# Delta rule's inverse in a two-layer recurrent kernel: each head in its own row half, products on the two diagonal quarters of TensorE, one transpose per level on VectorE

## The chip, the cores and the metric

The kernel runs on one core of a Trainium2 chip. The time is that of the whole kernel on the device, in microseconds (us). Before the change it is 2453.71 us, the median of three runs (2449.43, 2453.71, 2456.01).

## What is computed

Two layers of a mixer work on 1280 tokens (256 of context, 1024 of the latent) of width 1024. The change is in one stage of the first layer, the recurrence called rwkv: 8 heads of 64 channels, each with a 64x64 state that is decayed, corrected by a rank-one term and extended at every token, once forward and once backward over the tokens. The part of the reference:

```python
def rwkv_scan(inputs, S):
    def step(S, xs):
        r, v, kk, w, k, a = xs
        sa = jnp.einsum('bhvk,bhk->bhv', S, -kk)
        S = S * w[:, :, None, :] + sa[..., None] * (kk * a)[:, :, None, :] + v[..., None] * k[:, :, None, :]
        return S, jnp.einsum('bhvk,bhk->bhv', S, r)
    S, ys = lax.scan(step, S, tuple(jnp.moveaxis(t, 2, 0) for t in inputs))
    return jnp.moveaxis(ys, 0, 2), S
```

## The kernel before

The kernel doesn't step token by token. It cuts the tokens into 20 chunks of 64 (`C = 64`), and for each chunk, head and direction it forms a 64x64 strictly triangular matrix of key products, and needs the inverse of the identity plus that matrix. With the inverse a whole chunk is solved by one product per head. Two directions by 20 chunks give 40 steps; two steps (lanes 0 and 1) make a block, so `stage_rwkv_scan` (from L1540) runs over `B = 20` blocks. The 8 heads are `J = 4` pairs: head `q = 0` of a pair has its channels and chunk rows in partitions 0 to 63, head `q = 1` in 64 to 127. A block so holds 2 lanes x 4 pairs x 2 = 16 inverses of 64x64, all float32.

**The inverse by levels.** The inverse is grown in place in the tile `inv`. GpSimd sets blocks of two tokens (`begin_inverse`, L1990, four instructions a block). Then five levels (`TOP = 5`, `n` from 1 to 5) join neighbouring blocks of 2^n tokens into blocks of twice the size. A level is:

1. `half_product` (L1833) on TensorE: for each of the 16 inverses the strict matrix (`strict_t`, stationary, 64x64) times the 32 columns of the inverse that are to change (moving, 64x32). ScalarE copies the result from PSUM to the tile `half` (`copy_half`, L1903).
2. Beside it, `turn_inverse` on VectorE transposes the present inverse within blocks of 32x32 into the tile `lower` (L2047, L2049).
3. `upper_product` (L1842) on TensorE: `lower` (stationary, 64x64) times `half` (moving, 64x32).
4. `merge_upper` (L2055) on VectorE writes the result from PSUM into `inv` where a mask has ones. Only then may the next level's `half_product` and `turn_inverse` begin.

**Where the heads lie.** A matmul with 64 rows and 64 columns uses one quarter of the array: the rows are those of its operands' partitions, the columns those of its output's partitions. Before the change `inv` has a side index (`(j % 2) ^ q`), heads are taken two pairs at a time (`fours`), and the list `quarters` sends four consecutive matmuls to the four quarters: two of them keep the row half, two cross to the other one. `half` and `lower` hold heads in the crossed half between the two products, and `turn_inverse` has three instructions: one over 128 partitions for the side that stays, and two over 64 partitions that move the other side to the opposite half. The products lie in two PSUM banks, 32 of every 128 columns.

**The order of the work.** Each engine's order is written out by hand, and engines wait on semaphores. On TensorE the two products of a level have other work between them: the previous block's chunks (`begin_chunk` L1789, `solve_chunk` L1798, `begin_outputs` L1807, `update` L1815, `end_outputs` L1821), the next block's products (`strict_products` L1732, `products` L1743), `pull` (L1780), and transposes (`turn_keys` L1755, `turn_v` L1770). ScalarE has the copies out of PSUM (`copy_half`, `copy_u` L1926, `copy_y` L1943, and others), VectorE the masked products (`read_products` L2039), `add_rest` (L2064) and `update_state` (L2072, L2073). `update` waits for `copy_u`, which waits for `solve_chunk`. SyncE loads the next blocks' operands as the levels go by, waiting for `half_ready` and `upper_ready`.

A float32 matmul stands in the trace as two weight loads and two matmuls, so 16 matmuls are 32 rows of each kind.

Of the kernel before, what the change touches and what calls it, by code (L numbers as in the profile page):

```python
# [19 lines left out]
P = 128  # L20
# [559 lines left out]
R_LEVELS = 6  # L580
# [959 lines left out]
def stage_rwkv_scan(p, arena, operands, v_dram, shared, spare, own, chunk_decay, y, next_weights, free, bonus_dram):  # L1540
# [55 lines left out]
    with ExitStack() as local:  # L1596
# [4 lines left out]
        strict_t = sb("strict_t", [P, 2, 2, J, C])  # L1601
        inv = sb("inv", [P, 2, 2, 2, J // 2, C])
        lower = sb("lower", [P, 2, J, C])
        half = sb("half", [P, 2, J, C // 2])
        rest, pulled = sb("rest", [P, J, C]), sb("pulled", [P, 2, J, C])
# [14 lines left out]
            [P, 2 * J, C >> (n + 1), 1 << n])  # L1620
        identity = column(0, 5 + R_LEVELS).unsqueeze(1).broadcast_to([P, 2, J // 2, C])
        PAIR, KEYS, TURN, STRICT, CHAIN, OUT = 0, (2, 5), 3, 5, 6, 7
# [4 lines left out]
        flat = lambda a: a.rearrange("p l j n -> p (l j) n")  # L1627
        fours = [(lane, jj) for lane in range(2) for jj in range(J // 2)]
        quarters = [(0, 0), (1, 1), (0, 1), (1, 0)]
        four = lambda lane, jj: lane * (J // 2) + jj  # L1630
        own_inverse = lambda b, lane, j, q: inv[part(q), b % 2, (j % 2) ^ q, lane, j // 2, :]
        pair_bank = lambda which, lane, jj: bank(PAIR + which)[:, four(lane, jj) * P:four(lane, jj) * P + C // 2]
        pair_banks = p.psum[:, PAIR:PAIR + 2, :].rearrange("p r (f n) -> p (r f) n", n=P)[:, :, 0:C // 2]
        with nc.Block() as block:
# [88 lines left out]
            def _(pe):  # L1723
# [101 lines left out]
                def half_product(b, n):  # L1825
                    if n == 1:
                        pe.wait_ge(strict_read, 2 * (b + 1))
                        pe.wait_ge(level0_ready, 4 * (b + 1))
                    if b or n > 1:
                        pe.wait_ge(upper_merged, TOP * b + n - 1)  # L1830
                    for lane, jj in fours:
                        for q, r in quarters:
                            last = nc.tensor.matmul(pair_bank(q, lane, jj)[part(r)], strict_t[part(q), b % 2, lane, 2 * jj + r, :],  # L1833
                                                    changed(own_inverse(b, lane, 2 * jj + r, q), direction(b), n), start=True, stop=True)
                    last.then_inc(half_ready, 1)

                def upper_product(b, n):
                    pe.wait_ge(lower_turned, TOP * b + n)
                    pe.wait_ge(half_copied, TOP * b + n)
                    for lane, jj in fours:  # L1840
                        for q, r in quarters:
                            last = nc.tensor.matmul(pair_bank(q ^ r, lane, jj)[part(q)], lower[part(r), q ^ r, four(lane, jj), :],  # L1842
                                                    half[part(r), q, four(lane, jj), :], start=True, stop=True)
                    last.then_inc(upper_ready, 1)
# [53 lines left out]
            def _(act):  # L1898
                def copy_half(b, n):
                    act.wait_ge(half_ready, TOP * b + n)  # L1900
                    if b or n > 1:
                        act.wait_ge(upper_ready, TOP * b + n - 1)
                    nc.scalar.copy(half[:, :, :, :].rearrange("p q f n -> p (q f) n"), pair_banks).then_inc(half_copied, 1)  # L1903

# [74 lines left out]
            def _(pool):  # L1979
                begun, added = [0], [0]  # L1980

                def begin_inverse(b, lane, q):
# [3 lines left out]
                    if begun[0] >= 2:  # L1986
                        pool.wait_ge(level0_ready, begun[0] - 1)
                    begun[0] += 1
                    pairs = prod[part(q), b % 2, lane, q, :, part(q)].rearrange("p (j r) n -> p r j n", r=2)
                    nc.gpsimd.tensor_tensor(inv[part(q), b % 2, :, lane], pairs if q == 0 else pairs[:, ::-1],  # L1990
                                            identity[part(q)], ALU.add).then_inc(level0_ready, 1)
# [34 lines left out]
            def _(dve):  # L2026
# [14 lines left out]
                def turn_inverse(b, n):  # L2041
                    if n == 1:
                        dve.wait_ge(level0_ready, 4 * (b + 1))
                    if b or n > 1:
                        dve.wait_ge(upper_merged, TOP * b + n - 1)
                    here = inv[:, b % 2].rearrange("p s l j n -> p s (l j) n")
                    nc.vector.transpose(lower[:, 0], here[:, 0])  # L2047
                    for q in range(2):
                        last = nc.vector.transpose(lower[part(1 - q), 1], here[part(q), 1])  # L2049
                    last.then_inc(lower_turned, 1)  # L2050

                def merge_upper(b, n):
                    dve.wait_ge(upper_ready, TOP * b + n)
                    whole = inv[:, b % 2].rearrange("p s l j (g t w) -> p (s l j) g t w", t=2, w=1 << n)
                    nc.vector.copy_predicated(whole[:, :, :, 1 - direction(b)], added_to_pairs(direction(b), n),  # L2055
                                              pair_banks.rearrange("p f (g w) -> p f g w", w=1 << n)).then_inc(upper_merged, 1)

# [1898 lines left out]
```

## Time and profile before

| what | value |
|---|---|
| median of three runs | 2453.71 us |
| profiled execution, its own time | 2456.63 us |
| span of its core, first to last instruction | 2454.8 us |
| mean granted TensorE clock | 0.970 of full speed |
| TensorE busy (matmul) | 2294.7 us, 93% |
| VectorE busy | 1320.0 us, 54% |
| ScalarE busy | 794.4 us, 32% |
| GpSimd busy | 251.0 us, 10% |

The stage of the change runs from about 925 to 1305 us of the span. Busy time counts overlapping instructions once, and a matmul's row lasts from its start to its last result, so a TensorE that is busy need not start a matmul at its fastest rate. PE is TensorE's matmul, PEld its weight load, DVE VectorE, ACT ScalarE, POOL GpSimd. "issue" as the reason of a wait is idle time for which the profile shows no releaser. L1833 is line 1833 of the kernel.

### The profile page before, as it was taken

The page shows a single profiled execution, that of the slowest core. Times are in us where ns is not written, and L with a number is a line of the kernel's source. Part 1 is how long each engine was busy: PE and PEld are TensorE (multiplying, and loading weights), DVE is VectorE, ACT ScalarE, POOL GpSimd, SP SyncE. Part 2 cuts the span into 40 slices and gives each one's busy share as a digit, 9 for nine tenths or more (in the row PEclk, how much of TensorE's full clock was granted, in tenths as well). Part 3 has the DMA queues.
Part 4 walks back from the last instruction along what each step waited for, and adds up shares of the span by engine and source line. Part 5 has one row for each costly group of instructions (what it writes and reads, how often), then busy time and mean ns, then how long its engine had stood idle before and what let it go on. Part 6 is the DMA issues. An engine that isn't in the chain of part 4 may idle for free. (4 is left out here: it accounts for less than half of the span.)

```text
span 2454.8 us, 50670 instructions
## 1 busy us (share of the span) xinstructions
PE 2294.7 (93%) x22140; PEld 1417.6 (58%) x22140; DVE 1320.0 (54%) x2181; ACT 794.4 (32%) x1533; POOL 251.0 (10%) x280
## 2 busy tenths in 40 slices
PE   6999999999989988888887998999998999999898
PEld 4444456666644447887784443444685666756443
DVE  3320335553348756777774454555395666667514
ACT  4121222224455653443232222110101445465411
POOL 0000000000002211111221102341100000000000
PEclk8999999999989998999999998999999999999999
DMA  8100122122056654433325422111122100000233
GB/s 332 60 19 7 43 78 76 63 66 73 19 154 145 172 155 112 118 94 95 90 61 196 138 98 76 47 47 34 69 104 80 36 27 27 28 18 10 96 97 117
DMA packets 131866, 207.29 MB, mean 84 GB/s; under 512 B 15629, under 2 KB 95245, under 8 KB 128062
## 3 DMA queue, kind: packets, MB, share of 16 engines
q1 hardware_dynamic: 118398, 154.74, 20.2%
q0 software_dynamic: 13248, 49.32, 7.0%
q8 instruction: 175, 2.87, 0.5%
q14 instruction: 45, 0.37, 0.1%
HBM read 154.01 MB, written 50.01 MB: 83 GB/s over the span
## 5 line engine op out<-in xcount | busy, mean ns | idle before, releaser
L737 PE MATMUL psum<-arena,shared 128*128 128x512 f32 (+1 forms) x864 | 328.3, 524 | 1.5 <-PEq L223 1.5
L2861 PE MATMUL psum<-arena,second_shared 128*128 128x512 f32 (+1 forms) x640 | 282.3, 568 | 11.1 <-PEq L3682 6.4
L737 PEld LDWEIGHTS psum<-arena,shared 128*128 128x128 f32 x864 | 156.9, 191 | 108.5 <-issue 101.5
L2861 PEld LDWEIGHTS psum<-arena,second_shared 128*128 128x128 f32 x640 | 112.4, 195 | 77.0 <-issue 71.8
L1243 PE MATMUL psum<-shared,arena 128*128 128x512 f32 x320 | 150.0, 618 | 0.0
L2247 PE MATMUL psum<-shared,fin_mix 128*128 128x512 f32 x320 | 143.4, 601 | 2.9 <-POOL fin_mix L2380 2.9
L2247 PEld LDWEIGHTS psum<-shared,fin_mix 128*128 128x128 f32 x320 | 59.8, 192 | 75.0 <-issue 71.5
L1243 PEld LDWEIGHTS psum<-shared,arena 128*128 128x128 f32 x320 | 60.3, 196 | 73.3 <-issue 72.9
L841 ACT ACTIVATE shared<-psum 128x512 f32<-128x512 f32 (+1 forms) x48 | 25.2, 525 | 216.2 <-PE psum L737 216.2
L1842 PE MATMUL psum<-r_half,r_lower 64*64 64x32 f32 x3200 | 78.6, 225 | 13.5 <-issue 11.2
L1903 ACT COPY r_half<-psum 128x256 f32<-128x256 f32 x100 | 37.3, 373 | 162.0 <-PE psum L1833 161.7
L2049 DVE STREAM_TRANSPOSE r_lower<-r_inv 64x256 f32<-64x256 f32 x200 | 87.9, 440 | 2.7
L1990 POOL TENSOR_TENSOR r_inv<-r_prod,shared 64x256 f32<-64x256 f32 x80 | 58.0, 724 | 291.2 <-PE psum L1798 184.2
L1833 PE MATMUL psum<-r_inv,r_strict_t 64*64 64x32 f32 x3200 | 73.9, 225 | 14.6 <-issue 10.9
L330 PE MATMUL psum<-arena,shared 128*128 128x512 f32 (+3 forms) x240 | 87.4, 523 | 0.0
L3146 DVE TENSOR_TENSOR arena<-arena,g_k 128x512 f32<-128x512 f32 x56 | 39.6, 706 | 87.4 <-ACT arena L3014 87.4
L3014 ACT ACTIVATE arena<-arena 128x1024 f32<-128x1024 f32 x64 | 69.4, 1084 | 34.6 <-DVE arena L3127 32.8
L2852 PE MATMUL psum<-second_shared,arena 128*128 128x128 f32 x640 | 80.3, 277 | 0.0
L1833 PEld LDWEIGHTS psum<-r_inv,r_strict_t 64*64 64x64 f32 x3200 | 61.5, 138 | 27.1 <-issue 16.9
L1842 PEld LDWEIGHTS psum<-r_half,r_lower 64*64 64x64 f32 x3200 | 65.9, 139 | 18.7 <-issue 13.0
L2055 DVE COPY_PREDICATED r_inv<-shared,psum 128x256 f32<-128x256 uint32 x100 | 49.6, 496 | 50.2 <-PE psum L1842 49.0
L2852 PEld LDWEIGHTS psum<-second_shared,arena 128*128 128x128 f32 x640 | 75.1, 192 | 1.1 <-issue 0.5
(457 smaller groups left out, 4257.6 us busy)
## 6 DMA issues: line engine op xcount, KB each, us to landing
arena<-scratch_operands SPq DMA_DIRECT2D x152, 128.0 KB, 2.7
shared<-in_l_w_in SPq DMA_DIRECT2D x22, 512.0 KB, 4.0
scratch_spill<-shared POOLq DMA_DIRECT2D x16, 640.0 KB, 3.2
second_shared<-in_l_w_in SPq DMA_DIRECT2D x20, 512.0 KB, 3.9
scratch_operands<-arena POOLq DMA_DIRECT2D x14, 640.0 KB, 8.3
scratch_operands<-arena POOLq DMA_DIRECT2D x28, 320.0 KB, 11.3
shared<-in_l_mod_w SPq DMA_DIRECT2D x8, 1024.0 KB, 9.4
t_matrix<-in_transform SPq DMA_DIRECT2D x8, 1024.0 KB, 4.9
```

What stands on the lines that cost most here:

```text
L330: last = nc.tensor.matmul(p.psum[0:rows_out, bank_of[u], 0:width], lhsT, rhs, start=(k == 0), stop=(k == KT - 1))
L737: last = nc.tensor.matmul(p.psum[:, FILL + f % BANKS, 0:width], weight[:, q % PIECES, k, :], hT[:, k, at:at + width], start=(k == 0), stop ...
L1243: last = nc.tensor.matmul(p.psum[:, PROJECT + u % 2, :], hT[:, k, t * P:(t + 1) * P], weight[:, job, k, :], start=(k == 0), stop=(k == KT ...
L1833: last = nc.tensor.matmul(pair_bank(q, lane, jj)[part(r)], strict_t[part(q), b % 2, lane, 2 * jj + r, :], changed(own_inverse(b, lane, 2 * ...
L1842: last = nc.tensor.matmul(pair_bank(q ^ r, lane, jj)[part(q)], lower[part(r), q ^ r, four(lane, jj), :], half[part(r), q, four(lane, jj), ...
L1990: nc.gpsimd.tensor_tensor(inv[part(q), b % 2, :, lane], pairs if q == 0 else pairs[:, ::-1], identity[part(q)], ALU.add).then_inc(level0_r ...
L2049: last = nc.vector.transpose(lower[part(1 - q), 1], here[part(q), 1])
L2055: nc.vector.copy_predicated(whole[:, :, :, 1 - direction(b)], added_to_pairs(direction(b), n), pair_banks.rearrange("p f (g w) -> p f g w" ...
L2247: last = nc.tensor.matmul(p.psum[:, OUT + 2 * (t % 2) + n, :], mixed[:, t % SLOTS, k, :], weight[:, k, n * BANK:(n + 1) * BANK], start=(k ...
L2852: last = nc.tensor.matmul(bank[:, (t - part[0]) * P:(t - part[0] + 1) * P], hT[:, kk, t * P:(t + 1) * P], w[:, kk, :], start=(kk == 0), st ...
L2861: last = nc.tensor.matmul(bank[:, 0:width], w[:, kk, :], hT[:, kk, first:first + width], start=(kk == 0), stop=(kk == KT - 1))
L3014: nc.scalar.activation(out, out, ACT.Exp).then_inc(sig["exps_ready"], 1)
```

## The change

`inv`, `lower` and `half` lose the side index and hold each head in its own row half. `half_product` and `upper_product` run over the 8 combinations of lane and pair and over `q`, so consecutive matmuls alternate between the two diagonal quarters; their number and shapes stay the same. The first product's results lie in the first 256 columns of PSUM bank 0, the second's in the other 256 columns. `turn_inverse` is one instruction over 128 partitions and 512 columns. `begin_inverse`, `copy_half` and `merge_upper` move the same number of elements as before with plainer addresses. The order on every engine and all waits stay.

```diff
--- before.py
+++ after.py
@@ -1599,9 +1599,9 @@
         queries, keys = (lambda s: window[:, s % SLOTS, 0]), (lambda s: window[:, s % SLOTS, 1])
         prod = sb("prod", [P, 2, 2, 2, J, 2 * C])
         strict_t = sb("strict_t", [P, 2, 2, J, C])
-        inv = sb("inv", [P, 2, 2, 2, J // 2, C])
-        lower = sb("lower", [P, 2, J, C])
-        half = sb("half", [P, 2, J, C // 2])
+        inv = sb("inv", [P, 2, 2, J, C])
+        lower = sb("lower", [P, 2 * J, C])
+        half = sb("half", [P, 2 * J, C // 2])
         rest, pulled = sb("rest", [P, J, C]), sb("pulled", [P, 2, J, C])
         k_tok = sb("k_tok", [P, 2, J, P])
         CHUNK = 2 * J * C
@@ -1618,19 +1618,17 @@
         changed = lambda a, d, n: a.rearrange("p (g t w) -> p g t w", t=2, w=1 << n)[:, :, 1 - d]
         added_to_pairs = lambda d, n: changed(own[:, d, (5 + n) * C:(6 + n) * C], d, n).unsqueeze(1).bitcast(U32).broadcast_to(
             [P, 2 * J, C >> (n + 1), 1 << n])
-        identity = column(0, 5 + R_LEVELS).unsqueeze(1).broadcast_to([P, 2, J // 2, C])
+        identity = column(0, 5 + R_LEVELS).broadcast_to([P, J, C])
         PAIR, KEYS, TURN, STRICT, CHAIN, OUT = 0, (2, 5), 3, 5, 6, 7
         bank = lambda b: p.psum[:, b, :]
         narrow = lambda a: a.rearrange("p (j n) -> p j n", n=C)
         paired = lambda a: a.rearrange("p (j n) -> p j n", n=P)
         at = lambda lane, j: slice((lane * J + j) * C, (lane * J + j + 1) * C)
         flat = lambda a: a.rearrange("p l j n -> p (l j) n")
-        fours = [(lane, jj) for lane in range(2) for jj in range(J // 2)]
-        quarters = [(0, 0), (1, 1), (0, 1), (1, 0)]
-        four = lambda lane, jj: lane * (J // 2) + jj
-        own_inverse = lambda b, lane, j, q: inv[part(q), b % 2, (j % 2) ^ q, lane, j // 2, :]
-        pair_bank = lambda which, lane, jj: bank(PAIR + which)[:, four(lane, jj) * P:four(lane, jj) * P + C // 2]
-        pair_banks = p.psum[:, PAIR:PAIR + 2, :].rearrange("p r (f n) -> p (r f) n", n=P)[:, :, 0:C // 2]
+        heads = [(lane, j) for lane in range(2) for j in range(J)]
+        own_inverse = lambda b, lane, j, q: inv[part(q), b % 2, lane, j, :]
+        narrowed = lambda where, lane, j: slice(where * HALF + (lane * J + j) * C // 2, where * HALF + (lane * J + j + 1) * C // 2)
+        products_of = lambda where: bank(PAIR)[:, where * HALF:(where + 1) * HALF]
         with nc.Block() as block:
             @block.sync
             def _(sp):
@@ -1828,19 +1826,19 @@
                         pe.wait_ge(level0_ready, 4 * (b + 1))
                     if b or n > 1:
                         pe.wait_ge(upper_merged, TOP * b + n - 1)
-                    for lane, jj in fours:
-                        for q, r in quarters:
-                            last = nc.tensor.matmul(pair_bank(q, lane, jj)[part(r)], strict_t[part(q), b % 2, lane, 2 * jj + r, :],
-                                                    changed(own_inverse(b, lane, 2 * jj + r, q), direction(b), n), start=True, stop=True)
+                    for lane, j in heads:
+                        for q in range(2):
+                            last = nc.tensor.matmul(bank(PAIR)[part(q), narrowed(0, lane, j)], strict_t[part(q), b % 2, lane, j, :],
+                                                    changed(own_inverse(b, lane, j, q), direction(b), n), start=True, stop=True)
                     last.then_inc(half_ready, 1)
 
                 def upper_product(b, n):
                     pe.wait_ge(lower_turned, TOP * b + n)
                     pe.wait_ge(half_copied, TOP * b + n)
-                    for lane, jj in fours:
-                        for q, r in quarters:
-                            last = nc.tensor.matmul(pair_bank(q ^ r, lane, jj)[part(q)], lower[part(r), q ^ r, four(lane, jj), :],
-                                                    half[part(r), q, four(lane, jj), :], start=True, stop=True)
+                    for lane, j in heads:
+                        for q in range(2):
+                            last = nc.tensor.matmul(bank(PAIR)[part(q), narrowed(1, lane, j)], lower[part(q), lane * J + j, :],
+                                                    half[part(q), lane * J + j, :], start=True, stop=True)
                     last.then_inc(upper_ready, 1)
 
                 for lane in range(2):
@@ -1900,7 +1898,7 @@
                     act.wait_ge(half_ready, TOP * b + n)
                     if b or n > 1:
                         act.wait_ge(upper_ready, TOP * b + n - 1)
-                    nc.scalar.copy(half[:, :, :, :].rearrange("p q f n -> p (q f) n"), pair_banks).then_inc(half_copied, 1)
+                    nc.scalar.copy(half[:, :, :].rearrange("p f n -> p (f n)"), products_of(0)).then_inc(half_copied, 1)
 
                 def copy_keys(b, lane):
                     act.wait_ge(keys_turned, 2 * b + lane + 1)
@@ -1986,8 +1984,7 @@
                     if begun[0] >= 2:
                         pool.wait_ge(level0_ready, begun[0] - 1)
                     begun[0] += 1
-                    pairs = prod[part(q), b % 2, lane, q, :, part(q)].rearrange("p (j r) n -> p r j n", r=2)
-                    nc.gpsimd.tensor_tensor(inv[part(q), b % 2, :, lane], pairs if q == 0 else pairs[:, ::-1],
+                    nc.gpsimd.tensor_tensor(inv[part(q), b % 2, lane], prod[part(q), b % 2, lane, q, :, part(q)],
                                             identity[part(q)], ALU.add).then_inc(level0_ready, 1)
 
                 def add_y(b, lane):
@@ -2043,17 +2040,14 @@
                         dve.wait_ge(level0_ready, 4 * (b + 1))
                     if b or n > 1:
                         dve.wait_ge(upper_merged, TOP * b + n - 1)
-                    here = inv[:, b % 2].rearrange("p s l j n -> p s (l j) n")
-                    nc.vector.transpose(lower[:, 0], here[:, 0])
-                    for q in range(2):
-                        last = nc.vector.transpose(lower[part(1 - q), 1], here[part(q), 1])
-                    last.then_inc(lower_turned, 1)
+                    nc.vector.transpose(lower[:, :, :].rearrange("p f n -> p (f n)"),
+                                        inv[:, b % 2].rearrange("p l j n -> p (l j n)")).then_inc(lower_turned, 1)
 
                 def merge_upper(b, n):
                     dve.wait_ge(upper_ready, TOP * b + n)
-                    whole = inv[:, b % 2].rearrange("p s l j (g t w) -> p (s l j) g t w", t=2, w=1 << n)
+                    whole = inv[:, b % 2].rearrange("p l j (g t w) -> p (l j) g t w", t=2, w=1 << n)
                     nc.vector.copy_predicated(whole[:, :, :, 1 - direction(b)], added_to_pairs(direction(b), n),
-                                              pair_banks.rearrange("p f (g w) -> p f g w", w=1 << n)).then_inc(upper_merged, 1)
+                                              products_of(1).rearrange("p (f g w) -> p f g w", g=C >> (n + 1), w=1 << n)).then_inc(upper_merged, 1)
 
                 def add_rest(b, lane):
                     s = 2 * b + lane
```

## Rows read from the trace of the kernel before

**Rows 1.** Windows of the span: start:end us, length, busy us (x instructions), granted clock, DMA share, GB/s
```profile
core 0: us, PE busy (x) PEld busy (x) DVE busy (x) ACT busy (x) POOL busy (x), PEclk, DMA share, GB/s
925.00:935.00 10.00, 8.48 (x210) 7.56 (x208) 5.82 (x12) 2.98 (x9) 0.65 (x2) 0.55 0.26 84
935.00:954.00 19.00, 17.17 (x531) 15.96 (x534) 12.78 (x27) 6.72 (x17) 2.33 (x4) 0.82 0.32 93
1011.00:1305.00 294.00, 256.15 (x9100) 236.28 (x9092) 218.28 (x464) 103.37 (x270) 56.57 (x78) 0.98 0.29 82
925.00:1305.00 380.00, 330.26 (x11542) 304.51 (x11540) 277.94 (x590) 135.47 (x353) 68.25 (x95) 0.97 0.33 89
```

**Rows 2.** Groups by line and shape, 925 to 1305 us
```profile
line engine op names shapes xcount | busy us, mean ns | idle before us <-releasers
L2049 DVE STREAM_TRANSPOSE r_lower<-r_inv 64x256 f32<-64x256 f32 x200 | 87.9, 440 | 2.7
L1842 PE MATMUL psum<-r_half,r_lower 64*64 64x32 f32 x3200 | 78.6, 225 | 13.5 <-issue 11.2 <-DVE r_lower L2049 1.6 <-ACT r_half L1903 0.6
L1833 PE MATMUL psum<-r_inv,r_strict_t 64*64 64x32 f32 x3200 | 73.9, 225 | 14.6 <-issue 10.9 <-DVE r_inv L2055 2.5
...
L2039 DVE TENSOR_TENSOR r_prod<-psum,shared 128x512 f32<-128x512 f32 x76 | 50.6, 687 | 1.5 <-PE psum L1743 0.3
L2055 DVE COPY_PREDICATED r_inv<-shared,psum 128x256 f32<-128x256 uint32 x100 | 49.6, 496 | 50.2 <-PE psum L1842 49.0
...
L2047 DVE STREAM_TRANSPOSE r_lower<-r_inv 128x256 f32<-128x256 f32 x100 | 44.4, 444 | 12.0 <-POOL r_inv L1990 9.1 <-DVE r_inv L2055 0.5
L1903 ACT COPY r_half<-psum 128x256 f32<-128x256 f32 x100 | 37.3, 373 | 162.0 <-PE psum L1833 161.7
...
L1732 PE MATMUL psum<-arena 64*64 64x64 f32 x608 | 25.8, 223 | 0.4 <-issue 0.4
...
L1934 ACT COPY r_strict_t<-psum 128x256 f32<-128x256 f32 x38 | 14.2, 374 | 0.8
```

**Rows 3.** Who TensorE waited for, 925 to 1305 us: total, times, longest
```profile
PE psum L1842 <- issue: 11.2, 14, 2.4
PE psum L1833 <- issue: 10.9, 15, 1.6
PE psum L1815 <- issue: 5.2, 6, 1.3
PE psum L1815 <- ACT shared L1926: 4.1, 9, 0.5
PE psum L1807 <- issue: 3.6, 4, 1.3
PE psum L1815 <- ACT r_uv L1926: 2.9, 6, 0.5
PE psum L1833 <- DVE r_inv L2055: 2.5, 4, 0.9
PE psum L1821 <- issue: 2.4, 4, 0.9
PE psum L1798 <- issue: 2.0, 2, 1.0
PE psum L1842 <- DVE r_lower L2049: 1.6, 3, 1.2
```

**Rows 4.** One level in order of time, all engines: start, length, group
```profile
983.19 0.67 PE L1833 MATMUL psum<-r_inv,r_strict_t 64*64 64x32 f32 x32
983.42 0.89 DVE L2049 STREAM_TRANSPOSE r_lower<-r_inv 64x256 f32<-64x256 f32 x2
...
983.92 0.37 ACT L1903 COPY r_half<-psum 128x256 f32<-128x256 f32 x1 [0.43 <-PE psum L1833]
...
984.87 0.25 PE L1842 MATMUL psum<-r_half,r_lower 64*64 64x32 f32 x3
...
985.65 0.73 DVE L2055 COPY_PREDICATED r_inv<-shared,psum 128x256 f32<-128x256 uint32 x1 [0.52 <-PE psum L1842]
```

**Rows 5.** TensorE alone in order of time, two stretches of the next levels
```profile
987.04 0.45 PE L1815 MATMUL psum<-shared,r_k_tok 128*64 128x64 f32 x6
988.78 0.51 PE L1815 MATMUL psum<-shared,r_k_tok 128*64 128x64 f32 x10 [1.30 <-issue]
989.07 0.69 PE L1821 MATMUL psum<-shared,r_prod 128*64 128x64 f32 x16
989.69 0.67 PE L1842 MATMUL psum<-r_half,r_lower 64*64 64x32 f32 x32
990.28 1.16 PE L1743 MATMUL psum<-arena 64*128 64x128 f32 x16
991.38 0.67 PE L1833 MATMUL psum<-r_inv,r_strict_t 64*64 64x32 f32 x32
991.86 0.66 PE L1732 MATMUL psum<-arena 64*64 64x64 f32 x16
...
995.36 0.69 PE L1815 MATMUL psum<-shared,r_k_tok 128*64 128x64 f32 x16 [0.46 <-ACT shared L1926]
```

**Rows 6.** TensorE in another stage, a wide weight with two moving columns
```profile
744.35 2.29 PE L1272 MATMUL psum<-consts,gp_grown 128*128 128x2 f32 x20
```

**Rows 7.** DMA queue that brings instructions, 925 to 1305 us
```profile
q8 instruction: 92, 1.51, 1.7%
```

## The prediction, made before the changed kernel was run

> **What bounds the kernel now.** The windows come first. From 925 to 1305 us TensorE's matmul rows cover 330.3 of 380 us, VectorE's 277.9, ScalarE's 135.5 and GpSimd's 68.3 [rows 1]. In this stage TensorE has 50 us in which nothing ran on it, VectorE 102 us. The question is who waits for whom. The list of TensorE's waits says it: 35.9 us of its idle time have no releaser but "issue" (11.2 + 10.9 + 5.2 + 3.6 + 2.4 + 2.0, and 0.6 in rows too small to show), 7.0 us are the wait of `update` for ScalarE's copy of u (4.1 + 2.9), and VectorE is named for 1.6 us through `lower` and 2.5 us through `inv` [rows 3]. VectorE in turn idles 49.0 us ahead of its 100 merges, waiting for `upper_product`, and ScalarE 161.7 us ahead of `copy_half`, waiting for `half_product` [rows 2]. So TensorE's order of work sets the stage, and the others follow it.
>
> One level in order of time shows why. The half products begin at 983.19. The three transposes are over at 983.42 + 0.89 = 984.31, and the copy of the half at 983.92 + 0.37 = 984.29. The upper products begin only at 984.87, as TensorE is at the work that stands between [rows 4]. Both inputs had waited for 0.56 us.
>
> **The transposes.** Now they are 445 ns over 128 partitions and twice 440 ns over 64 [rows 2]: the length goes by columns, not by partitions. Three make 1.33 us a level. The trace has no transpose of 512 columns. From below it costs no less than one of 256, 445 ns; from above no more than two, 890 ns. The nearest row is the masked product over 128x512, 687 ns, which is a VectorE instruction of the same width, so I take 0.7 us. That takes 0.6 us x 100 = 63 us from VectorE. By the level above it brings TensorE nothing: the end of the transposes moves from 984.31 to about 983.7, where no one waits for it. What it can bring at most is the 1.6 us and 2.5 us that TensorE waited for VectorE [rows 3]. I take 0, since with slower products in between these waits are covered too.
>
> **The copies, merges and GpSimd.** `copy_half` reads 32 of every 128 columns of two banks and takes 373 ns; the copy of a strict product, the same size in one contiguous piece, takes 374 ns [rows 2]. The plain address brings nothing. `merge_upper` has a mean of 496 ns, and 0.73 us at level 1, where it writes runs of two elements [rows 2, 4]. The runs are as before. From below I bound it by the 440 ns of a 256-column instruction (-6 us over the stage if all of it were on the path), from above by 0.73 us (+23 us); I take 0, as count, size and runs don't change. `begin_inverse` has the same sizes, and GpSimd is idle for most of the stage.
>
> **The products.** This is the term that decides. The 3200 rows of each of L1833 and L1842 remain, but two quarters take the place of four. The rows show the rate: 32 rows of L1833 take 0.67 us from first start to last end, and one lasts 0.22 us, so a row starts every (0.67 - 0.22) / 31 = 14.5 ns, four quarters in 58 ns [rows 2, 5]. The strict products of L1732 run on the two diagonal quarters, with the same 64x64 weights and 64 moving columns: 16 rows take 0.66 us, so one starts every (0.66 - 0.22) / 15 = 29.3 ns, two quarters in 59 ns [rows 2, 5]. A round takes as long with 32 moving columns on four quarters as with 64 on two. What is common to both is the weight, so a quarter seems to take a new weight every 58 ns, and the 32 moving columns hide behind it.
>
> A row from elsewhere checks this. L1272 loads 128x128 weights and moves only two columns: 20 rows in 2.29 us, which is (2.29 - 0.25) / 19 = 107 ns each (0.25 us being my estimate for the last row's length, from the 0.22 above) [rows 6]. With nothing to move, 128 columns of weight cost 107 ns; half as many should cost some 54 ns, near the 58 seen. One more way to read the four quarters would be that two of them share the rows and so stream their 32 columns in turn. L1821 has 64 moving columns on two column halves over the same 128 rows: (0.69 - 0.22) / 15 = 31 ns a row, 63 ns for the pair [rows 5]. They run side by side, so that reading fails.
>
> From below, then, the changed products cost what they do now, 14.5 ns a row; from above the 29.3 ns of L1732. I take 29.3, since it is the same pair of quarters and the same weight. Each of the 200 product groups gets 31 x 14.8 = 0.46 us longer: 92 us in all.
>
> The Trainium skill has a rule that speaks against this change more strongly. Its page "TensorEngine Tiling (Array Packing)", section "Restrictions and Gotchas", says that different row tiles cannot access the same PSUM bank at the same time, and the change puts both row halves into bank 0. By that rule the two quarters would take turns, a row every 58 ns. The trace disagrees: the strict products of both row halves go to one bank as well, and start every 29.3 ns. I keep it as a rival.
>
> **The cold clock.** The granted clock is 0.55 in the first 10 us and 0.82 in the 19 after it, so TensorE runs at 1.2 GHz for about 9 + 7 = 16 us [rows 1]. Some 0.9 x 210 + 0.36 x 531 = 380 rows fall there, more than half of them, some 210, of the changed products; at half the clock each loses another 14.8 ns: +3 us. Whether the rest of the stage keeps its 0.98 is open; I take it that it does.
>
> **What absorbs a part.** First, the wait of `update` for u. In the second half of a block TensorE runs `solve_chunk`, then `half_product`, then waits for ScalarE's copies before `update`; the row at 995.36 has 0.46 us of it [rows 5]. A half product longer by 0.46 us fills it: -7.0 us [rows 3]. Second, the unexplained stalls: 1.30 us in the middle of `update`, between two rows of one line that wait for nothing [rows 5]. Instructions come over a DMA queue, 92 fetches of 16 KB in the stage, one for about 125 matmul rows (11542 / 92) [rows 1, 7]. If a stall is TensorE using up its instructions before the next fetch has landed, a slower TensorE stalls less. Not at all is one end (0 us), wholly the other (-35.9 us). About half of all rows are of the changed lines (6400 of 11542), so a run of about 60 rows that ends in a stall takes about 0.4 us longer; the 45 stalls that the rows count would give up to 18 us. I take half of 35.9, -18 us. Third, every other place: between a half and an upper product the fill was longer than copy and transposes, so no idle time takes up the extra 0.46 us; between an upper product and the next level the merge starts after the product's end and moves with it.
>
> **The sum**, against the profiled execution's own time of 2456.6 us: +92 + 3 - 7 - 18 = +70, so 2526.6 us. That execution stands 2.9 us above the median, so for the median I say 2524 us, 2.9% slower.
>
> **Its range.** Low: a pitch of 27 ns instead of 29.3 gives 31 x 12.5 x 200 = 78 us; all stalls and the wait gone: 78 - 43 = +35, about 2489. High: nothing of the stalls absorbed and the merges a bit slower, +92 + 3 - 7 + 10 = +98, about 2552. The likely part is 2498 to 2550.
>
> **Rivals.**
> - *The pitch is that of a stream of instructions, not of a quarter's weight.* Then two quarters take a row every 14.5 ns, the products cost the same, and only VectorE's saving is left. For it: 32 columns are half of L1732's 64, so nothing shows 32 columns on two quarters. Against it: L1272, and that the round is 58 ns in both. Time: at best the 1.6 + 2.5 us of waits for VectorE, and a third of the 9.1 us that VectorE waits for GpSimd [rows 2], if earlier transposes pull that forward: 2447 to 2453. This is the rival on the other side. It decides from the point at which a changed row's pitch stays under about 18 ns: below it the 200 groups add no more than 31 x 3.5 ns x 200 = 22 us, which the stalls and the wait could swallow.
> - *TensorE's idle time takes more.* The stage's idle time is 50 us in all. If it takes nearly all of that, +42: 2496; with the short pitch of 27 ns 2480 to 2490.
> - *The two row halves exclude each other in one bank.* A row every 58 ns: 200 x 31 x 44 ns = 273 us, of which at most 43 us is absorbed: 2684 to 2727.
> - *The clock falls.* Fewer quarters at work, and the granted clock spends more of the stage at 1.2 GHz. Against it: the stage's clock is 0.98 with TensorE busy for 87% [rows 1]. Each 10% of the stage at the lower level costs up to half of 10% of 380 us, some 19 us: 2545 to 2570.
>
> **Chances.** Forecast 0.79, TensorE's idle time takes more 0.08, pitch unchanged 0.07, clock 0.04, bank 0.02. A range of 2492 to 2552 leaves out the bank, the unchanged pitch, and parts of two others. A measurement of this kernel tells about 0.3% (7 us) from no change. The unchanged pitch splits between faster and no change, with 2447 at its edge: faster 0.04, same 0.05, slower 0.91.
>
> **What would show it.** In the changed profile 32 rows of each product line take about 1.13 us instead of 0.67. The transpose is one row of about 0.7 us. `issue` waits fall to about half, the wait of L1815 for the copy of u goes away, VectorE's busy time in the stage falls by about 60 us to some 215, and its idle time ahead of the merges grows. The stage lasts about 450 us instead of 380. I am wrong if 32 rows still take under 0.75 us, if the upper products wait for `half`, or if the stage's clock is below 0.93.

## The result and the profile after

The changed kernel takes 2480.06 us, the median of four runs (2478.92 to 2481.68), against 2453.72 us before. The ratio is 1.011 with a 95% interval of 1.0092 to 1.0127: slower by 26 us. The prediction had the direction but not the size: 2524 us, with a range of 2492 to 2552 that does not hold 2480. The profiled execution's span is 2479.9 us, 25.1 more than before.

First, the stage of the change. This is the kernel before in two windows, from the first half product's start to the last one's, and from there to the end (columns as in [rows 1]):

```profile
925.30:1300.40 375.10, 325.89 (x11421) 300.73 (x11420) 276.03 (x587) 133.07 (x347) 67.43 (x93) 0.97 0.33 90
1300.40:2454.80 1154.40, 1083.70 (x7612) 630.14 (x7604) 631.24 (x934) 330.31 (x537) 117.76 (x94) 0.97 0.22 71
```

And the same two windows of the changed kernel (within 0.2 us):

```profile
927.00:1327.40 400.40, 395.25 (x11430) 375.12 (x11428) 212.66 (x388) 132.96 (x347) 67.33 (x93) 0.98 0.31 84
1327.40:2479.90 1152.50, 1082.22 (x7598) 629.27 (x7588) 630.54 (x932) 329.70 (x537) 115.47 (x94) 0.98 0.22 72
```

All of the difference is in the stage: 375.1 us became 400.4, +25.3, and what follows is the same within 2 us. In the stage TensorE sat idle for 375.1 - 325.9 = 49.2 us before and for 400.4 - 395.3 = 5.2 us after. VectorE's busy time fell by 63 us.

The groups by line of the changed kernel, 925 to 1330 us, which answer to [rows 2]:

```profile
L1831 PE MATMUL psum<-r_inv,r_strict_t 64*64 64x32 f32 x3200 | 115.1, 223 | 4.0 <-DVE r_inv L2049 2.4 <-issue 0.5 <-POOL r_inv L1987 0.4
L1840 PE MATMUL psum<-r_half,r_lower 64*64 64x32 f32 x3200 | 113.3, 222 | 1.4 <-ACT r_half L1901 1.1
...
L2043 DVE STREAM_TRANSPOSE r_lower<-r_inv 128x512 f32<-128x512 f32 x100 | 70.9, 709 | 5.1 <-POOL r_inv L1987 1.0
...
L2049 DVE COPY_PREDICATED r_inv<-shared,psum 128x256 f32<-128x256 uint32 x100 | 49.4, 494 | 94.1 <-PE psum L1840 94.1
L1901 ACT COPY r_half<-psum 128x256 f32<-128x256 f32 x100 | 37.2, 372 | 184.4 <-PE psum L1831 184.4
```

The transpose is one row of 709 ns. Copy and merge have the length they had. VectorE now idles 94.1 us ahead of its merges instead of 49.0. Who TensorE waited for, complete, which answers to [rows 3]:

```profile
PE psum L1831 <- DVE r_inv L2049: 2.4, 4, 0.8
PE psum L1768 <- DVE r_prod L2036: 1.5, 1, 1.5
PE psum L1840 <- ACT r_half L1901: 1.1, 2, 0.6
PE psum L1831 <- issue: 0.5, 1, 0.5
PE psum L1831 <- POOL r_inv L1987: 0.4, 1, 0.4
```

The stalls that had no releaser, 35.9 us in 47 places, are down to 0.5 us in one. The wait for the copy of u (7.0 us) is gone. TensorE alone in order of time, which answers to [rows 5]:

```profile
996.55 1.12 PE L1831 MATMUL psum<-r_inv,r_strict_t 64*64 64x32 f32 x32
997.60 0.69 PE L1813 MATMUL psum<-shared,r_k_tok 128*64 128x64 f32 x16
998.12 0.64 PE L1819 MATMUL psum<-shared,r_prod 128*64 128x64 f32 x16
998.68 1.12 PE L1840 MATMUL psum<-r_half,r_lower 64*64 64x32 f32 x32
999.74 1.16 PE L1741 MATMUL psum<-arena 64*128 64x128 f32 x16
```

Product groups of 32 rows last 1.12 us instead of 0.67, (1.12 - 0.22) / 31 = 29 ns a row. `update` (L1813) has its 16 rows without a break, and the next group begins before the last results of the one ahead are out.

### The profile page after: what moved, and what is told of

Same layout as the page of the kernel before. It is cut to its first block and busy times, and to the rows that moved or that the text cites. A ratio compares the mean times of both kernels' runs of the same rounds, so it can differ in the third digit from the quotient of the medians.

```text
span 2479.9 us, 50470 instructions
## 1 busy us (share of the span) xinstructions
PE 2362.4 (95%) x22140; PEld 1492.5 (60%) x22140; DVE 1256.0 (51%) x1981; ACT 793.4 (32%) x1533; POOL 248.4 (10%) x280
## 5 line engine op out<-in xcount | busy, mean ns | idle before, releaser
L2855 PE MATMUL psum<-arena,second_shared 128*128 128x512 f32 (+1 forms) x640 | 282.6, 568 | 10.9 <-PEq L3676 6.4
L1831 PE MATMUL psum<-r_inv,r_strict_t 64*64 64x32 f32 x3200 | 115.1, 223 | 4.0 <-DVE r_inv L2049 2.4
L1840 PE MATMUL psum<-r_half,r_lower 64*64 64x32 f32 x3200 | 113.3, 222 | 1.4 <-ACT r_half L1901 1.1
L1831 PEld LDWEIGHTS psum<-r_inv,r_strict_t 64*64 64x64 f32 x3200 | 103.8, 137 | 16.9 <-DVE r_inv L2049 6.1
L1840 PEld LDWEIGHTS psum<-r_half,r_lower 64*64 64x64 f32 x3200 | 104.7, 138 | 4.6 <-issue 1.8
L2049 DVE COPY_PREDICATED r_inv<-shared,psum 128x256 f32<-128x256 uint32 x100 | 49.4, 494 | 94.1 <-PE psum L1840 94.1
L3426 PE MATMUL psum<-arena,yf_weight 128*128 128x512 f32 x168 | 74.4, 592 | 0.0
## 6 DMA issues: line engine op xcount, KB each, us to landing
scratch_operands<-arena POOLq DMA_DIRECT2D x28, 320.0 KB, 10.9
```

Source lines behind the costliest of these rows:

```text
L1831: last = nc.tensor.matmul(bank(PAIR)[part(q), narrowed(0, lane, j)], strict_t[part(q), b % 2, lane, j, :], changed(own_inverse(b, lane, j, ...
L1840: last = nc.tensor.matmul(bank(PAIR)[part(q), narrowed(1, lane, j)], lower[part(q), lane * J + j, :], half[part(q), lane * J + j, :], star ...
L2855: last = nc.tensor.matmul(bank[:, 0:width], w[:, kk, :], hT[:, kk, first:first + width], start=(kk == 0), stop=(kk == KT - 1))
L3426: last = nc.tensor.matmul(bank(made), left[:, k, :], right[:, k, :], start=(k == 0), stop=(k == HALF - 1))
```

## The experiments

The theory after the result: the slower rows are the whole cost (+92 us of TensorE's time), VectorE's gain is worth nothing, and the kernel before was held back by something that slower rows hide. I take that to be the supply of instructions, the fetches of [rows 7]. The rivals: the shorter transpose saved the difference of 44 us to the forecast; the new places of the data matter; the rate of a row is not that of its weight; the stalls are chance.

**One: two quarters at a time, all else as before.** In the kernel before, both products get another order:

```diff
-                    for lane, jj in fours:
-                        for q, r in quarters:
+                    for lane, jj, two in [(lane, jj, two) for two in (quarters[0:2], quarters[2:4]) for lane, jj in fours]:
+                        for q, r in two:
```

> The kernel before, with its heads, tiles and three transposes as they are; only the order inside both products is another: first the 16 matmuls' eight on the two diagonal quarters, then the eight on the two crossed ones, so that two quarters are in use at a time and not four. Theory (the number of quarters in use sets the rate, and nothing else of the change matters): a row starts every 29 ns in both product lines, 32 rows take 1.12 us, and the time is that of the changed kernel, 2480 us, within 4. Rival (the new places in PSUM or the crossing of the halves matter too): the rate changes but the time lies clearly off 2480, under 2470 if VectorE's shorter transpose had cost the changed kernel something by its collisions, over 2485 if the shorter transpose had brought it something.

Measured: 2460.41 us, ratio 1.0031 (1.0014 to 1.0048). The theory's number missed. The time lies in the rival's range, but as the edit did less than I meant, it decides between neither:

```profile
982.53 0.92 PE L1842 MATMUL psum<-r_half,r_lower 64*64 64x32 f32 x32
983.39 1.16 PE L1743 MATMUL psum<-arena 64*128 64x128 f32 x16
984.48 0.92 PE L1833 MATMUL psum<-r_inv,r_strict_t 64*64 64x32 f32 x32
```

A group lasts 0.92 us, not 1.12: (0.92 - 0.22) / 31 = 23 ns a row (21 to 23 over the groups). In one group's starts the first 10 rows come in pairs 58 to 59 ns apart, as with two quarters; from 266 ns on further pairs come in between, before 16 rows have started. So the crossed quarters begin while the diagonal ones still run. TensorE has some 0.2 to 0.25 us more a group, 40 to 50 us in all, and the kernel is 5 to 8 us slower. Its stalls with no releaser fell to 14.2 us in 26 places.

**Two: the same in `half_product` alone.**

> As the run before, but only half_product has the two-and-two order; upper_product keeps four quarters. Theory (slower rows cost in proportion, part of each hidden by stalls that go): half of the change's 26 us, 2463 to 2471 us. Rival (the stalls swallow a first portion whole, and only what exceeds them shows): the first 100 of the 200 slower product groups cost nearly nothing, 2453 to 2460 us.

Measured: 2456.02 us, ratio 1.0001 (0.9983 to 1.0019). The time is the rival's, though the edit added only half of what I meant: the first 20 to 25 us of extra TensorE time cost nothing, within the interval's 5 us. The stalls are 21.5 us in 35 places.

**Three: the changed kernel with three transposes.**

```diff
-                    nc.vector.transpose(lower[:, :, :].rearrange("p f n -> p (f n)"),
-                                        inv[:, b % 2].rearrange("p l j n -> p (l j n)")).then_inc(lower_turned, 1)
+                    here = inv[:, b % 2]
+                    nc.vector.transpose(lower[:, 0:J, :].rearrange("p f n -> p (f n)"), here[:, 0].rearrange("p j n -> p (j n)"))
+                    for q in range(2):
+                        last = nc.vector.transpose(lower[part(q), J:, :].rearrange("p f n -> p (f n)"),
+                                                   here[part(q), 1].rearrange("p j n -> p (j n)"))
+                    last.then_inc(lower_turned, 1)
```

> The changed kernel with its one transpose over 128x512 cut back into three, one over 128x256 and two over 64x256, all within their own row half. VectorE's busy time in the stage grows by 0.62 us x 100. Theory (VectorE waits for TensorE and nobody for the transpose): 2480 us within 3. Rival (the shorter transpose is what kept the cost down to 26 us instead of the 70 forecast): 2490 to 2520 us.

Measured: 2481.93 us, ratio to the kernel before 1.0116 (1.0081 to 1.0152), the changed kernel's own 1.011. The interval alone would allow some 9 us either way. The stage of the profiled execution is closer: 400.1 us for 400.4, with VectorE 52 us busier. The transposes' length does not matter there.

**Four: the kernel before with one transpose.** Its `turn_inverse` becomes one instruction over all 512 columns.

> The kernel before with one transpose over 128x512 a level in place of its three. The move of half the blocks to the other row half is left out, so those heads get other heads' data. TensorE's work is that of the kernel before. Theory (the transpose is not on the path): 2454 us within 4. Rival (VectorE's load holds the stage back through merges and masked products): 2430 to 2447 us.

Measured: 2451.55 us, ratio 0.9982 (0.9967 to 0.9997). So 61 us of VectorE's time are worth some 4 us here, by the interval 1 to 8. That is not quite nothing, but the rival that VectorE holds the stage back falls.

**Five: the layout of before, but diagonal quarters only.** The matmuls that crossed over take both operands from the row half of their output:

```diff
-                                matmul(pair_bank(q, lane, jj)[part(r)], strict_t[part(q), b % 2, lane, 2 * jj + r, :],
-                                                    changed(own_inverse(b, lane, 2 * jj + r, q), direction(b), n)
+                                matmul(pair_bank(q, lane, jj)[part(r)], strict_t[part(r), b % 2, lane, 2 * jj + r, :],
+                                                    changed(inv[part(r), b % 2, q ^ r, lane, jj, :], direction(b), n)
-                                matmul(pair_bank(q ^ r, lane, jj)[part(q)], lower[part(r), q ^ r, four(lane, jj), :], half[part(r), q, ...
+                                matmul(pair_bank(q ^ r, lane, jj)[part(q)], lower[part(q), q ^ r, four(lane, jj), :], half[part(q), q, ...
```

> The kernel before with its layout, its two PSUM banks and its three transposes, but all products on the two diagonal quarters: those that crossed over take their operands from the row half of their output, so half the heads get other heads' data. The order in two passes of an earlier run let the queue overlap diagonal and crossed quarters (21 ns a row); here only two quarters exist. Theory (the two quarters are the whole cost of the change): a row every 29 ns and the changed kernel's 2480 us, within 5. Rival (part of the 26 us comes from the new places of the data, one PSUM bank above all): 2460 to 2470 us.

Measured: 2486.07 us, ratio 1.0106 (1.0076 to 1.0137), the same as the change's 1.011 (the kernel before had 2457.66 us beside it). A row starts every 29.1 ns. Three transposes, two PSUM banks and the old places are all there; only the quarters differ. That is the whole cost of the change, shown by itself within the interval. Stalls with no releaser: 0.5 us.

**Six: all 64 columns moved** in the changed kernel's `half_product`, into bank 1:

```diff
-bank(PAIR)[part(q), narrowed(0, lane, j)], strict_t[...], changed(own_inverse(b, lane, j, q), direction(b), n)
+bank(PAIR + 1)[part(q), at(lane, j)], strict_t[...], own_inverse(b, lane, j, q)
-nc.scalar.copy(half[:, :, :].rearrange("p f n -> p (f n)"), products_of(0))
+nc.scalar.copy(half[:, :, :].rearrange("p f (g w) -> p (f g) w", w=1 << n), changed(bank(PAIR + 1), direction(b), n))
```

> The changed kernel, whose half_product moves all 64 columns of the inverse instead of the 32 that change (into PSUM bank 1; the copy takes the 32 that are needed, from strided places). Theory (a quarter's rate is that of its 64-column weight, and up to 64 moving columns hide behind it): a row still starts every 29 ns, and the time is 2480 us within 3, a little more if the strided copy is slower. Rival (the moving columns set the rate on two quarters): twice the columns give some 55 ns a row, 31 x 26 ns x 100 = +80 us, 2560.

Measured: 2478.55 us, ratio 1.0088 (1.0065 to 1.011).

```profile
991.87 1.15 PE L1831 MATMUL psum<-r_inv,r_strict_t 64*64 64x64 f32 x32
```

Twice the moving columns, and the group lasts 1.15 us for 1.12, 30 ns a row. So up to 64 the moving columns are not what sets the rate. What is left is the 64-column weight, 58 ns for each in its quarter. No run here changed the weight's width in these products; What speaks for it is [rows 6], with twice the weight columns and only two moving ones: its rows start 112 ns apart (the prediction's 107 averages in a first pair 29 ns apart). The Trainium skill says in "TensorE: Matmul & The Clock Gate", section "LDWEIGHTS (loading the stationary operand)", that a load takes the number of columns over 1.2 GHz, whatever the rows, an estimate of 53 ns for 64. The pace in the traces is some 5 ns above that; a weight load's own row lasts 135 ns, so the trace does not show the load by itself.

**Seven and eight: more rows in both kernels.** In the kernel before the loop of both products becomes `for lane, jj in fours + fours[0:2]`, in the changed one `for lane, j in heads + heads[0:J]`: half of each group's matmuls are issued twice.

> The kernel before, with the first eight matmuls of every product group issued a second time at its end, on all four quarters, with the same result: 16 more rows in each of 200 groups, 160 a block. At 14.5 ns a row these are 46 us of TensorE's own time. Theory (the kernel before is held back by the supply of instructions: about half of its stage lies in runs of rows that are short against the 2.5 us from one fetch's start to the end of its stall): each row costs the supply's 32 ns or so, not its own 14.5, and the time grows by 75 to 100 us, to 2530 to 2555. Rival (the stalls are chance, or belong to something else that does not grow with the number of instructions): the rows cost their own time, +40 to +50, 2494 to 2504 us.

> The changed kernel with the first eight matmuls of every product group issued a second time, 16 more rows in each of 200 groups. At 29.1 ns a row they are 93 us of TensorE's own time. Theory (with two quarters in use TensorE is slower than the supply and works without gaps): each row costs its own 29 ns, +90 to +100 us, 2570 to 2580, nearly the same increase as the same rows bring to the kernel before. Rival (supply plays no part in either): +93 here and only half of that there.

Measured: in the kernel before +83.5 us (2539.95 against 2456.43, ratio 1.0339, 1.0313 to 1.0366); in the changed one 2582.11 us, ratio 1.0508 (1.048 to 1.0536), which is 98 us over the change by the ratios and 102 by the medians. This is the test that separates best. The 3200 added rows of the trace, 16 in each of 200 groups, have 46 us of own time in the kernel before at 14.5 ns, and cost 83.5, 26 ns each. In the changed kernel they have 93 us of own time and cost about 100, 31 ns each. A part of both increases is a lower granted clock in these executions: half the time at 1.2 GHz, which is the most that it can cost, is 18.8 us of the stage for 12.9 without the rows, and 17.3 for 8.5. Without it the added rows cost some 24 ns each in the kernel before and 28 in the changed one. Where the rows are fast, they pay for something beyond their own time. The waits of TensorE in the kernel before with more rows:

```profile
PE psum L1842 <- issue: 20.7, 28, 1.5
PE psum L1833 <- issue: 19.1, 24, 1.5
PE psum L1798 <- issue: 7.1, 5, 1.9
PE psum L1807 <- issue: 6.1, 4, 1.7
```

All rows of that kind together are 63.2 us in 82 places, for 35.9 in 47 before: 28% more rows, 76% more stall time. The changed kernel with more rows has 0.3 us of them.

What the stalls wait for can be read from the times of the instruction fetches [rows 7]. In the kernel before, every one of the 47 stalls ends 2.2 to 3.8 us after the latest fetch began, half of them within 2.7 us. Moments picked evenly over the stage lie 0 to 6.3 us behind the latest fetch, a tenth of them less than 0.4 us. With more rows the 82 stalls end 2.1 to 3.2 us after one. So the ends of the stalls are tied to the fetches.

**Nine and ten: fewer rows.** `begin_chunk` and `begin_outputs` move the same state. They become one product with a 64x128 weight, 16 rows for 32, twice a block:

```diff
-                        last = nc.tensor.matmul(bank(CHAIN)[part(q), at(0, j)], queries(s)[part(q), j, q, :], state[part(q), j, :],
-                                                start=True, stop=True)
+                        last = nc.tensor.matmul(out_bank(q)[:, at(0, j)], queries(s)[part(q), j].rearrange("p k t -> p (k t)"),
+                                                state[part(q), j, :], start=True, stop=True)
```

with `out_bank` bank 7 or 2, two half copies of the output's first part on ScalarE, one more addition a step on GpSimd, `add_rest` in two halves, and `strict_products` behind `solve_chunk`.

> The kernel before, with begin_chunk and begin_outputs made one: the same state is moved through a 64x128 weight instead of twice through a 64x64 one, so a block has 32 matmul rows fewer of about 600, at the same array time (16 rows at 59 ns for 32 at 29). The first part of the output no longer accumulates with the second in PSUM; ScalarE copies both and GpSimd adds them. strict_products moves behind solve_chunk. The result is the same. Theory (the kernel before is held back by the supply of instructions): 640 rows less at 26 to 31 ns each, -15 to -20 us, 2434 to 2442 us. Rival (the array's time or the chain of a level holds it back): no change, 2450 to 2460 us.

> The same merging of begin_chunk and begin_outputs in the changed kernel. Theory (there TensorE's array time is the bound, and it does not change): 2474 to 2484 us. Rival (the number of instructions still decides): -15 to -20 us, 2460 to 2465.

Measured: on the kernel before 2455.39 us, ratio 0.999 (0.9977 to 1.0002), no gain, which is the rival's range. On the changed kernel it is 2505.71 us, ratio 1.0189 (1.0168 to 1.021), 26 us over the changed kernel by the medians and 19 by the ratios, outside both ranges. The theory's expectation missed in both. The array time was not the same. The changed kernel with it:

```profile
997.16 1.12 PE L1832 MATMUL psum<-r_inv,r_strict_t 64*64 64x32 f32 x32
998.21 1.11 PE L1795 MATMUL psum<-r_state,arena 64*128 64x64 f32 x16
999.25 1.12 PE L1841 MATMUL psum<-r_half,r_lower 64*64 64x32 f32 x32
1000.27 0.68 PE L1804 MATMUL psum<-r_rest,r_inv 64*64 64x64 f32 x16
1000.79 0.63 PE L1734 MATMUL psum<-arena 64*64 64x64 f32 x16
```

The merged product has the 0.94 us of the two (16 rows at 59 ns), but the two did not lie one behind the other: `begin_outputs` is on the crossed quarters and `solve_chunk` on the diagonal ones, and they overlapped. In its place stands `strict_products`, on the same quarters as `solve_chunk`. And the group at 998.21 starts 0.07 us before the results ahead of it are out (997.16 + 1.12 = 998.28), where in the changed kernel the next group of the same shape starts 0.17 us before them:

```profile
992.73 1.12 PE L1831 MATMUL psum<-r_inv,r_strict_t 64*64 64x32 f32 x32
...
993.68 0.66 PE L1787 MATMUL psum<-r_state,arena 64*64 64x64 f32 x16
```

A change of weight shape costs some 0.1 us. The Trainium skill, "TensorEngine Tiling (Array Packing)", section "Tiling Modes", says that changing the mode drains TensorE. The traces agree in that it starts later, but by the profile's modelled ends the next group still starts 0.07 us before the last results.

The stages in the profiled executions, from the first half product to the last, the kernel before first and the changed one second, both with the merged product (columns as in [rows 1]):

```profile
927.40:1294.70 367.30, 337.26 (x10810) 308.67 (x10812) 293.96 (x624) 161.79 (x423) 94.55 (x130) 0.97 0.35 92
926.90:1346.90 420.00, 416.45 (x10818) 396.40 (x10820) 227.40 (x426) 163.03 (x423) 94.71 (x130) 0.96 0.30 80
```

In the changed kernel the stage is 19.6 us longer than without the merging. Up to 10 of them are a lower granted clock (half the time at 1.2 GHz is 18.8 us, for 8.5), and the part behind the stage is another 5.6 us longer. In the kernel before the stage is 7.8 us shorter and the part behind it 3.6 longer. There the stalls with no releaser fell from 35.9 to 10.9 us, but a new wait came in their place, `solve_chunk` (here L1806) for `add_rest` on VectorE (L2075), as `strict_products` no longer stands between them:

```profile
PE psum L1806 <- DVE r_rest L2075: 15.0, 39, 0.9
```

So this pair changed several things at once: the number of rows, the overlap of groups, the changes of weight shape and that wait. It does not confirm that fewer rows are worth their share of the supply. It doesn't refute it either. I had hoped here for a version faster than both kernels; it ties with the one before.

## Why the prediction was wrong

*The products* were right in mechanism and nearly in size: 29.1 ns a row and 1.12 us a group in the changed kernel. But in the kernel before, the upper products started a row every 15.9 ns (the median group) and not every 14.5. Over all rows the two lines gained 83.5 us, not 92. Experiment five shows that the quarters are the cause; six shows that it is not the moving columns, and leaves the weight.

*VectorE* was right: one transpose of 709 ns (0.7 forecast), 63 us saved. In the changed kernel nothing of it is in the time (experiment three); in the kernel before it would have been worth some 4 us (experiment four).

*Copies, merges, GpSimd, the PSUM bank* were right: 372 and 494 ns as before. The two row halves start 6 ns apart into the one bank, and a pair of rows every 58 ns, as they do into two banks in experiment five. The rule on shared banks, with its 2684 us, does not hold here.

*The wait of `update` for u* was right: 7.0 us, gone.

*The stalls* are the step that failed: "I take half of 35.9, -18 us." All of it went, 35.4 us. Had I taken it whole, the forecast would have been 2506. But even the end of my range, 43 us absorbed, was too small, and that is the second error in the same step: I took the list of idle times for the whole of what TensorE loses. A row counts as busy for 0.22 us after its start, so each of 47 stalls is some 0.2 us longer than its entry. The one that ends at 988.78 has 1.30 us in [rows 5]; the rows ahead of it end at 987.04 + 0.45 = 987.49, so the last of them started at 987.27, 1.5 us before. That makes about 35.4 + 9 for the stalls and 7.0 for u, some 52 us absorbed, not 25.

*The cold clock* had +3. Half the stage's time at 1.2 GHz, which is the most that the lower level takes, was 12.9 us before and 8.5 after. But experiment five, on the same two quarters, has 12.9 too, and experiment three 8.5. The difference is one between executions and can't be laid to the change.

The sum as measured, from the starts of all rows of the stage. I split each distance from one row's start to the next at 60 ns (120 ns for the 128-column weights): what is below is the pace of the rows, what is above is a stop. The pace of the two product lines took 83.5 us more and that of all other lines 6.5 less. The stops fell from 94.6 us to 43.0, 51.6 less. That is 83.5 - 6.5 - 51.6 = +25.4, the stage's difference of 25.3 but for rounding; the clock is inside these terms. So of the 45 us between the forecast's +70 and this, some 27 are stops that went beyond the 25 I had taken, 8 or 9 are the products, 6 or 7 the other lines, and 3 the clock's term.

Why all of it went: the 0.4 us that I let a run of 60 rows gain was too little, as the 47 stalls were 0.8 us each on the average. The rows of one whole fetch take some 0.9 us longer, an estimate (83.5 us over 92 fetches). The runs of rows as a series say more than the sum. The time by which TensorE's own rows were slowed, and what came of it:

| kernel | rows slowed by | stalls with no releaser | time over the kernel before |
|---|---|---|---|
| before | 0 | 35.9 us | 0 |
| two: half products in twos | 20 to 25 us | 21.5 us | 0 |
| one: both in twos | 40 to 50 us | 14.2 us | +5 to +8 us |
| changed | 84 to 91 us | 0.5 us | +26 us |
| five: diagonal only | 84 to 91 us | 0.5 us | +26 to +28 us |

The first 20 us are free, the next 20 nearly so, and of the last 40 or so about 20 show. That is a bound which gives way to another. Experiments seven and eight support that the first bound goes by the number of TensorE's instructions; nine was to confirm it and did not. That it is the arrival of the 16 KB fetches [rows 7] rests on the times of the 47 and 82 stall ends behind a fetch's start, and on stalls between two rows of one line that wait for nothing. It is not shown by an experiment: no run here changed the fetches themselves.

The prediction had named three signs of being wrong, and none came: the groups last 1.12 us, the upper products wait for `half` for 1.1 us in two places only, and the clock is 0.98. They watched the cost. What failed was the part absorbed, and the figures given for it, `issue` waits at half and a stage of 450 us, came out at 0.5 us and some 405.

## What to carry to other kernels

Small matmuls that each bring their own weight ran here at the pace of their part of the array, 58 ns each, and most likely the weight sets it, so count how many parts a sequence of them uses: going from four quarters to two doubled the time a row takes, and with two it was the same for 32 and for 64 moving columns. When an engine's idle time has no releaser, ask what its cause goes by before pricing a slower instruction at its full length: here some 84 us of extra array time cost 26. And a list of idle times is a lower bound of what an engine can absorb, since busy rows overlap its start.

## What the hardware showed that I had not expected

TensorE's matmuls on different quarters overlap although they are issued one behind the other: eight on two quarters and then eight on the other two gave 21 to 23 ns a row, between the 14.5 of four quarters and the 29 of two. And a stage of 11,421 recorded rows in 375 us, 33 ns a row, stalled 47 times for want, as it seems, of instructions, while single groups of it ran at 14.5 ns. Every one of these stalls ended 2.2 us or more after the latest fetch of instructions began.
